# HGRN core of a two-model block stack: query/key pairs rotated before they are normalised, and packed scores

## The chip, the cores and the metric

One core of one Trainium2 chip runs the whole program as one launch. The metric is the device time of a launch in microseconds. The kernel before took 2794.81 us (median of 3 runs, 2794.39 to 2797.06). One more execution was taken under the profiler; the rows in this document come from it.

## The reference, cut to what matters

The input is 512 tokens of 1024 channels. A first block (gated linear attention, a causal convolution, windowed attention, a feed-forward part) is followed by two layers of a second kind. The change touches only those two layers:

```python
for l in range(2):
    u = rmsnorm(x)
    q, k, v, qi, ki, wi, hq, hf, hi, hg, g_attn, g_hgrn = split(u @ w_in[l])
    q = rope(rmsnorm_per_head(q) * q_norm);  k = rope(rmsnorm_per_head(k) * k_norm)   # 8 heads of 64
    qi, ki = rope(qi), rope(ki)                                # 4 index heads, 1 index key head, of 64
    y_attn = sparse_attention(q, k, v, top 128 keys by sum_h wi_h * relu(qi_h . ki)) @ w_proj_attn
    # HGRN: 4 heads, S_t = diag(f_t) S_(t-1) + k_t v_t^T, o_t = S_t^T q_t
    y_hgrn = (rmsnorm(o) * hgrn_norm * silu(hg)) @ w_proj_hgrn
    x = x + (sigmoid(g_attn) * y_attn + sigmoid(g_hgrn) * y_hgrn) @ w_out
    x = x + ffn(x)
```

In the core of the HGRN, `A[t, s]` = sum over d of `q[t, d] k[s, d] exp(b[t, d] - b[s, d])` for s <= t, with `b` the running sum of the log decay. The norm of a head is a factor per token; a rotation turns the two halves of the head's channels into each other. So rotation and norm can change places, if the gain, which is per channel, is applied inside the rotation.

## The kernel before, in words

Activations are kept transposed, channels on partitions, tokens along the free dimension. Every product with weights is three fp32r matmuls for each 128 x 128 tile (high by high, high by low, low by high), so a panel of 1024 x 256 weights is 48 matmuls of 512 columns. The panels are a fixed list, `weight_panels` (line 180): SP loads panel p into `raw[p % 3]` when the results of panel p-3 are complete (line 874); ScalarE rounds it to `wh` (line 912, in `ahead`, which runs at fixed places of ScalarE's own program and waits for the load there); GpSimd makes `wl` (line 896). All engines run in-order programs written out by hand, and count semaphores.

**The core** (`core`: TensorE line 518, ScalarE line 1026, VectorE line 1493) has eight units, one for each pair of heads and block of 128 tokens. A unit is, in TensorE's order: sums of the log decays of one head (lines 543, 544), sums of the other, the turn of the next unit's logs (523), two transposes (556, to become `kdt` by a ScalarE copy at line 1044), score matmuls of seven levels and of the diagonal (567), the output product (575, 577), and the state product (581). ScalarE exponentiates the sums (1038). VectorE multiplies queries and keys into the decays, level by level (1521), then copies each level's scores under a mask into `attT` (1532), copies the output out (1536) and updates the state (1544). Level l splits the block into pieces of 128 / 2^(l+1) tokens, and only pieces with an odd number have queries of that level. The scores take three banks; level 6 and the diagonal go into the bank of levels 0 and 1, so TensorE waits there for the masked copies of those two.

Into these units a second program is dealt in steps, the side work (`side_core_2`: TensorE 768, ScalarE 1246, VectorE 1897). It has the same 40 steps on all three engines, and five a unit: one between the two sums, two behind the second sums, one behind the scores, one at the unit's end (`core_steps`, line 262; the slot between the sixth and seventh level is empty). On TensorE a step is a quarter of a panel, or a *thin* step:

```python
for j in range(4):                       # two pairs of query heads, two of key heads
    yield from project(uh, ul)           # four steps
    turn(qk_pair[j - 1]); yield          # if j > 0: rotation matrix times the normalised pair before
    mean of squares of pair j; yield
```

For pair j ScalarE copies and squares the projection, divides the sum, and takes logarithm and root in later steps; VectorE makes a Newton step on the root (`newton`, line 1607), multiplies pair and gain (1906) and makes the cosine part (`cosine`, 1803), then, after the turn, the sine part and the sum (`turned`, lines 1811 and 1814). The index queries and the index key with its weights follow, and the two value panels.

**After the core**, TensorE makes index scores, VectorE scores the keys (1830, 1832), and `core_post` (TensorE 644, ScalarE 1084, VectorE 1614) norms and gates the output in two halves. For each half TensorE projects a gate panel (`HG`), sums squares, and does four steps of `merge`; ScalarE takes the SiLU (1091) and the root; VectorE first does 14 rounds of the top-k selection (1842, 1844), then the norm (from 1609). Then attention begins with VectorE's masked logits (1652).

## Time and profile before

| | |
|---|---|
| median of the runs | 2794.81 us (2794.39 to 2797.06) |
| profiled execution | 2796.15 us |
| its span, first to last instruction | 2794.4 us |
| mean granted TensorE clock | 0.97 of 2.4 GHz |
| busy: TensorE, VectorE, ScalarE, GpSimd | 2626.1, 1172.5, 994.9, 1074.0 us |
| HGRN core of layers 0 and 1 | from 1039.1 and 1946.7 us, 196.9 and 198.9 us long |

TensorE's busy time contains the overlap of pipelined matmuls, so the time of a step is read from the start of its first matmul to the start of the next group. A busy share says little here; the waits and the windows say which engine was late.

### The profile page before, as it was taken

What the parts mean: (1) busy time and instruction counts of PE and PEld (TensorE: products, weight loads), DVE (VectorE), ACT (ScalarE), POOL (GpSimd) and SP (SyncE); (2) the same over time, 40 slices, a digit from 0 to 9 for tenths busy, and PEclk for the clock granted to TensorE, in tenths of its full rate; (3) what the DMA queues carried; (4) which work ended last, traced back from release to release, by engine and by line L of the source; (5) the groups of instructions that cost most, each with busy time, mean ns of one, the idle gap of its engine ahead of it and who ended that gap; (6) DMA issues with size and microseconds to landing.
All of it is one profiled execution on the core that took longest, in us unless ns stands there. A gap on an engine that the chain in (4) does not pass through costs nothing.

```text
span 2794.4 us, 30147 instructions
## 1 busy us (share of the span) xinstructions
PE 2626.1 (94%) x12478; PEld 2136.2 (76%) x12478; DVE 1172.5 (42%) x1924; ACT 994.9 (36%) x1152; POOL 1074.0 (38%) x816
## 2 busy tenths in 40 slices
PE   6999999999999979888999999999888899999999
PEld 5887777878888777776687888888767668788887
DVE  5243343365523546668625111133666772521112
ACT  3423443343323444425424222235432542432221
POOL 4323333544545442213244544543221324454452
PEclk8999999999999989999999999999999999999999
DMA  4222212222323221111122323223111212232232
GB/s 148 63 76 76 76 61 76 91 92 94 102 91 98 91 68 46 35 57 61 31 92 92 103 91 106 91 91 91 46 36 42 65 40 91 91 101 95 92 104 76
DMA packets 206707, 221.05 MB, mean 79 GB/s; under 512 B 3713, under 2 KB 197467, under 8 KB 206443
## 3 DMA queue, kind: packets, MB, share of 16 engines
q1 hardware_dynamic: 206064, 218.97, 24.5%
q8 instruction: 99, 1.62, 0.2%
q14 instruction: 37, 0.30, 0.0%
q10 hardware_dynamic: 507, 0.15, 0.0%
HBM read 217.01 MB, written 2.10 MB: 78 GB/s over the span
## 4 chain that ended last, share of the span: by engine, by line
PE 79%; DVE 12%; ACT 7%; DMA 1%; issue 1%; DVEq 0%; SPq 0%; ACTq 0%
PE psum L442 70%; PE psum L567 2%; ACT wh L912 2%; PE psum L684 1%; DVE dec L1521 1%; PE psum L672 1%; DMA raw<-in_w_in 1%; PE psum L663 1%; DVE score L1844 1%; DVE ul L1706 1%; DVE top L1842 1%; DVE ul L1417 1%; ACT dec L1038 1%; DVE merged L1729 1%; DVE normed L1478 1%
## 5 line engine op out<-in xcount | busy, mean ns | idle before, releaser
L896 POOL TENSOR_TENSOR wl<-raw,wh 128x512 fp32r<-128x512 f32 x812 | 1073.8, 1356 | 1694.4 <-ACT wh L912 1694.4
L442 PE MATMUL psum<-uh,wh 128*128 128x512 f32 x2024 | 811.8, 401 | 17.8 <-DVE ul L1706 4.4
L442 PE MATMUL psum<-ul,wh 128*128 128x512 f32 x2024 | 797.9, 394 | 0.0
L442 PE MATMUL psum<-uh,wl 128*128 128x512 f32 x2024 | 797.0, 394 | 0.0
L912 ACT CAST wh<-raw 128x2048 fp32r<-128x2048 f32 (+1 forms) x206 | 387.0, 1879 | 313.5 <-DMA raw<-in_w_ffn_out 117.6
L442 PEld LDWEIGHTS psum<-uh,wh 128*128 128x128 f32 x2024 | 386.8, 191 | 110.0 <-issue 14.5
L442 PEld LDWEIGHTS psum<-uh,wl 128*128 128x128 f32 x2024 | 385.9, 191 | 82.8
L442 PEld LDWEIGHTS psum<-ul,wh 128*128 128x128 f32 x2024 | 386.9, 191 | 79.0 <-issue 1.9
L442 PE MATMUL psum<-fh,wh 128*128 128x512 f32 x528 | 205.4, 389 | 0.0
L442 PE MATMUL psum<-fl,wh 128*128 128x512 f32 x528 | 205.4, 389 | 0.0
L442 PE MATMUL psum<-fh,wl 128*128 128x512 f32 x528 | 205.4, 389 | 0.0
L1748 DVE TENSOR_TENSOR xT<-xT,psum 128x1024 f32<-128x1024 f32 (+1 forms) x48 | 56.0, 1166 | 293.0 <-PE psum L442 292.8
L1794 DVE TENSOR_TENSOR tmp<-tmp,psum 128x1024 f32<-128x1024 f32 x22 | 26.9, 1221 | 358.5 <-PE psum L442 358.4
L442 PE MATMUL psum<-vh,wh 128*128 128x512 f32 x288 | 115.8, 402 | 9.2 <-DVE xT L1959 7.1
L442 PEld LDWEIGHTS psum<-fh,wl 128*128 128x128 f32 x528 | 99.1, 188 | 20.7
L442 PEld LDWEIGHTS psum<-fl,wh 128*128 128x128 f32 x528 | 99.1, 188 | 20.6
L442 PEld LDWEIGHTS psum<-fh,wh 128*128 128x128 f32 x528 | 99.1, 188 | 20.4
L442 PE MATMUL psum<-vh,wl 128*128 128x512 f32 x288 | 113.2, 393 | 0.0
L442 PE MATMUL psum<-wh,uh 128*128 128x256 f32 x320 | 92.6, 289 | 11.9 <-DVE ul L1417 11.9
L442 PE MATMUL psum<-vl,wh 128*128 128x512 f32 x256 | 99.7, 389 | 0.0
L567 PE MATMUL psum<-dec 128*128 128x128 f32 x448 | 66.0, 312 | 31.9 <-DVE attT L1532 18.6
L442 PE MATMUL psum<-brh,wh 128*128 128x512 f32 x224 | 94.2, 420 | 0.0
(314 smaller groups left out, 3343.7 us busy)
## 6 DMA issues: line engine op xcount, KB each, us to landing
raw<-in_w_in SPq DMA_DIRECT2D x78, 1024.0 KB, 5.2
raw<-in_w_ffn_in SPq DMA_DIRECT2D x44, 1024.0 KB, 5.1
raw<-in_w_up SPq DMA_DIRECT2D x22, 1024.0 KB, 5.1
raw<-in_w_ffn_out SPq DMA_DIRECT2D x16, 1024.0 KB, 5.1
raw<-in_w_down SPq DMA_DIRECT2D x8, 1024.0 KB, 5.0
raw<-in_w_out SPq DMA_DIRECT2D x8, 1024.0 KB, 5.1
raw<-in_w_ffn_out SPq DMA_DIRECT2D x8, 768.0 KB, 4.3
raw<-in_w_o SPq DMA_DIRECT2D x4, 1024.0 KB, 5.0
```

The lines of the kernel that those rows point to most:

```text
L442: ins = mm(dst, x, y, start=first and i == 0, stop=last and i == len(todo) - 1)
L567: ins = mm(X[1 + l // 2 % 3][:, c:c + P], lhs, rhs, start=True, stop=True)
L663: ins = mm(X[e][:, 0:(b1 - b0) * P], q[HD * e:HD * (e + 1), p, m * P:(m + 1) * P], kof(2 * p + e)[:, b0 * P:b1 * P], start=True, stop=True)
L672: ins = nc.tensor.transpose(X[2][:, b * P:(b + 1) * P], prob[i % 2][:, e, b * P:(b + 1) * P], ident)
L684: ins = mm(X[3][HD * e:HD * (e + 1), 0:P], vof(2 * p + e, b), probT[:, e, (b - b0) * P:(b - b0 + 1) * P], start=(b == b0), stop=(b == b1 - 1))
L896: ins = nc.gpsimd.tensor_tensor(wl[p % 3][:, w], raw[p % 3][:, w], wh[p % 3][:, w].bitcast(F32), ALU.subtract)
L912: nc.scalar.copy(wh[p % 3][:, 0:nk * width], raw[p % 3][:, 0:nk * width]).then_inc(S.hi_done, 1)
L1038: fn(dec[:, i, :, :].rearrange("p (b l) t -> p b (l t)", b=3), X4[:, 1:4, 0:3 * P], ACT.Exp).then_inc(S.dec_done, 1)
L1417: v.tensor_tensor(dst, src, high.bitcast(F32), ALU.subtract).then_inc(sem, 1)
L1478: v.scalar_tensor_tensor(normed[:, c % 2, :], xT[:, c, :], g(c), scale[:], ALU.mult, ALU.mult).then_inc(S.n_normed, 1)
L1521: ins = v.tensor_tensor(e[:, :, :, part, :], e[:, :, :, part, :], x[:, :, :, part, :], ALU.mult)
L1748: v.tensor_tensor(x, x, src, ALU.add).then_inc(pair_free[(n.q - 1) % 2], 1)
```

## The change

- The key-index panel is projected first in the side work, then the four pairs, the index queries, the two value panels, and as the last one the first of the two gate panels of `core_post`, which for these layers no longer projects it (`gated`); two of the four `merge` steps stand ahead of its first sum.
- A pair is handled unnormalised: ScalarE squares it (into a tile of its own, `qksq`) and copies it; one thin step on TensorE makes the mean of squares and the turn, the latter with a rotation matrix that has the gain multiplied in (`rot_gain`, made once a layer from a part of `const` that is no longer needed). VectorE takes the sine part in the step of the thin work, adds gain times cosine in the last step of a unit, and multiplies the root in the first step of the next.
- On ScalarE mean, weight cast, logarithm, root and square are one step (`rooted`).
- Scores of a level are computed for the odd pieces only, 64 columns for each head, and all eight results have places of their own in the three banks; the diagonal comes first; the masked copies go level by level to the odd pieces only. TensorE signals after levels 1, 3 and 6 and waits for all copies once.

```diff
-                  C_AQ, C_AQ + 256, C_AK, C_AK + 256, C_IQ, C_IK, C_AV, C_AV + 256, C_HG):
+                  C_IK, C_AQ, C_AQ + 256, C_AK, C_AK + 256, C_IQ, C_AV, C_AV + 256, C_HG):
-SIDE_CORE_2 = 4 * 6 + 4 + 4 + 2 * 4
+SIDE_CORE_2 = 2 + 4 * 5 + 4 + 5 + 5 + 4
+LEVEL_ENDS = (1, 3, 6)
+        def odd_blocks(x, l):
+            w = P >> (l + 1)
+            return x.rearrange("p (g two w) -> p g two w", two=2, w=w)[:, :, 1, :]
+        def level_scores(l):
+            w = P >> (l + 1)
+            at = l + 2 if l < 4 else l + 4
+            return X[1 + at // 4][:, P * (at % 4):P * (at % 4 + 1)].rearrange("p (h g w) -> p h g w", h=2, w=w)
 # TensorE, core
-                        if l == 6:
-                            take_on(side, core_steps(total, u, 2))
-                            pe.wait_ge(S.pairs_done, t.up(S.pairs_done))
...
+                    for i in range(2):
+                        h = 2 * hp + i
+                        ins = mm(X[1][:, i * P:(i + 1) * P], gk[:, h, tok], gq[:, h, tok], start=True, stop=True)
+                    for l in range(LEVELS):
+                        pe.wait_ge(S.lev_ready, t.up(S.lev_ready))
+                        for i in range(2):
+                            ins = mm(level_scores(l)[:, i, :, :], dec[:, i, l, :], odd_blocks(dec[:, i, l, :], l),
+                                     start=True, stop=True)
+                        if l in LEVEL_ENDS:
+                            ins.then_inc(S.att_done, 1)
 # TensorE, side work
+                yield from project(uh, ul, (0,))
+                keys = n.q - 1
                 for j in range(4):
                     yield from project(uh, ul)
                     mine = n.q - 1
-                    if j > 0:
-                        turn(qk_pair[j - 1])
-                        yield
                     dst = new_pair()
+                    pe.wait_ge(S.squared, t.up(S.squared))
+                    for i in range(2):
+                        ins = mm(dst[:, i, :], blk, qksq[:, i, :], start=True, stop=True)
+                    ins.then_inc(S.pair_full, 1)
                     pe.wait_ge(pair_free[mine % 2], mine // 2 + 1)
+                    turn(qk_pair[j], rot_gain[j // 2])
                     yield
 # ScalarE, side work
+                def squared(j):
                     src = next_pair()
...
+                    fn(qksq[:], src, ACT.Square).then_inc(S.squared, 1)
+                    fn(qk_pair[j], src, ACT.Copy).then_inc(pair_free[(n.q - 1) % 2], 1)
+                    ahead()
+                def rooted(j):
+                    src = next_pair()
+                    mean = n.q - 1
...
+                    mean_square(tmp[1][:], src, 1.0 / HD, pair_free[mean % 2])
+                    ahead()
+                    next_pair()
+                    ahead()
+                    act.wait_ge(pair_free[mean % 2], mean // 2 + 1)
+                    logarithm(tmp[0][:], tmp[1][:])
+                    inverse_root(tmp[0][:]).then_inc(S.r_root, 1)
+                yield from passed(2)
+                for j in range(4):
+                    yield from wait_steps(3)
+                    squared(j)
+                    yield
+                    rooted(j)
+                    yield
...
+                yield from wait_steps(3)
+                act.wait_ge(S.r_normed, t.up(S.r_normed))
+                silu_gate()
 # VectorE, core
-                        v.copy_predicated(attT[:], mask, src).then_inc(signal, 1)
+                        w = P >> (l + 1)
+                        mask = odd_blocks(pairmask[:, l, :], l).unsqueeze(1).to_broadcast([P, 2, P // (2 * w), w])
+                        dst = attT[:].rearrange("p h (g two w) -> p h g two w", two=2, w=w)[:, :, :, 1, :]
+                        v.copy_predicated(dst, mask, level_scores(l)).then_inc(signal, 1)
 # VectorE, side work
+                for j in range(4):
+                    next_pair()
+                    sine(tmp[2][:])          # sine table times the turned pair, from PSUM
+                    yield
+                    yield from wait_steps(2)
+                    cosines(j)               # pair * gain * cosine, then + sine part
+                    yield
+                    normed(j)                # newton(), then pair * root
+                    if j < 3:
+                        next_pair()
+                        yield
 # TensorE, core_post
+                    before = 2 if gated and j == 0 else 0
+                    take_on(side, before)
+                    if j or not gated:
+                        finish(project(uh, ul))
...
-                    take_on(side, side_steps[j])
+                    take_on(side, side_steps[j] - before)
```

## Rows read from the trace of the kernel before

**Rows 1.** Page, part 4: shares of the chain that ended last.
```profile
PE 79%; DVE 12%; ACT 7%; DMA 1%; issue 1%; DVEq 0%; SPq 0%; ACTq 0%
```
**Rows 2.** Windows (us; PE, PEld, DVE, ACT, POOL busy; PEclk): cores, units 3, 5, 0, stages after.
```profile
1039.10:1236.00 196.90, 174.77 (x970) 148.68 (x970) 117.68 (x265) 73.78 (x73) 47.53 (x36) 0.93 0.13 40
1946.70:2145.60 198.90, 174.96 (x969) 148.69 (x970) 118.49 (x265) 73.78 (x73) 47.48 (x36) 0.93 0.13 39
1111.10:1130.80 19.70, 19.43 (x105) 15.59 (x105) 13.66 (x34) 13.40 (x13) 5.31 (x4) 1.00 0.18 54
1156.20:1184.90 28.70, 22.29 (x113) 17.95 (x112) 17.49 (x36) 4.81 (x5) 6.93 (x4) 0.94 0.12 37
...
1039.10:1061.40 22.30, 21.07 (x107) 18.05 (x108) 8.47 (x28) 7.07 (x8) 4.19 (x4) 0.93 0.15 44
...
1236.00:1295.50 59.50, 50.68 (x220) 38.90 (x220) 47.07 (x108) 33.69 (x31) 15.20 (x12) 0.97 0.29 89
2145.60:2206.80 61.20, 52.40 (x221) 40.13 (x220) 47.04 (x107) 33.66 (x31) 15.21 (x12) 0.94 0.28 86
```
**Rows 3.** Waits of PE in the first core: total, times, longest.
```profile
PE psum L567 <- DVE attT L1532: 8.4, 3, 2.9
PE psum L567 <- DVE dec L1521: 6.7, 3, 2.4
PE psum L765 <- DVE ak L1906: 3.8, 1, 3.8
...
PE psum L779 <- ACT tmp L1266: 1.2, 1, 1.2
```
**Rows 4.** Timeline of PE in the first core: start us, us.
```profile
1051.44 3.29 PE L567 MATMUL psum<-dec 128*128 128x128 f32 x28
...
1054.93 0.48 PE L442 MATMUL psum<-uh,wh 128*128 128x512 f32 x1
...
1130.83 0.34 PE L543 MATMUL psum<-summask,lth 128*128 128x384 f32 x1
...
1131.89 0.39 PE L442 MATMUL psum<-uh,wh 128*128 128x512 f32 x1
...
1134.62 0.34 PE L543 MATMUL psum<-summask,lth 128*128 128x384 f32 x1
...
1207.58 0.36 PE L442 MATMUL psum<-wh,uh 128*128 128x256 f32 x1
...
1210.53 0.34 PE L543 MATMUL psum<-summask,lth 128*128 128x384 f32 x1
...
1211.67 0.41 PE L794 MATMUL psum<-const,tmp 4*128 4x4 f32 x4
```
**Rows 5.** Groups by form, ScalarE and VectorE: busy us, mean ns, idle before.
```profile
L912 ACT CAST wh<-raw 128x2048 fp32r<-128x2048 f32 x12 | 22.8, 1899 | 13.0 <-DMA raw<-in_w_in 13.0
L1038 ACT ACTIVATE dec<-psum 128x1152 f32<-128x1152 f32 x16 | 18.1, 1131 | 33.9 <-PE psum L544 33.8
L1075 ACT ACT_TABLE_LOAD x6 | 7.7, 1283 | 0.1
...
L1075 ACT ACTIVATE tmp<-tmp 128x1024 f32<-128x1024 f32 x6 | 6.4, 1061 | 0.1
...
L1532 DVE COPY_PREDICATED attT<-pairmask,psum 128x256 f32<-128x256 uint8 x64 | 28.5, 445 | 5.3 <-PE psum L567 3.4
...
L1521 DVE TENSOR_TENSOR dec<-dec,gk 128x128 f32<-128x128 f32 x56 | 15.8, 282 | 0.0
```
**Rows 6.** Page, part 6: a panel's DMA, median us from issue to landing.
```profile
raw<-in_w_in SPq DMA_DIRECT2D x78, 1024.0 KB, 5.2
```
**Rows 7.** Timeline of the stage after the first core.
```profile
1262.27 1.23 DVE L1609 TENSOR_TENSOR tmp<-tmp 128x1024 f32<-128x1024 f32 x1 [3.54 <-ACT tmp L1082]
...
1287.86 1.22 DVE L1609 TENSOR_TENSOR tmp<-tmp 128x1024 f32<-128x1024 f32 x1
...
1296.06 0.80 PE L663 MATMUL psum<-ak,aq 64*128 64x128 f32 x4 [7.01 <-DVE stat L1652]
```

More of the change, by code:

```diff
@@ L360, in build_program @@
         bias3 = at("bias3", 20, [P, 4 * P])
-        iwT = tmp[0][HD:HD + 4, 0, :]
+        iwT = at("iwT", 65, [P, T])[HD:HD + 4, :]
+        ikcos = at("ikcos", 67, [P, T])
+        qksq = at("qksq", 69, [P, 2, T])
+        rot_gain = [const[:, K_DIST + i * P:K_DIST + (i + 1) * P] for i in range(2)]
         prob = [tmp[0], tmp[1]]
@@ L783, in side_core_2 @@
                 queries = n.q - 1
-                turn(qk_pair[3])
-                yield
-                yield from project(uh, ul, (0,))
-                keys = n.q - 1
-                turn(iq, queries)
-                yield
-                yield from project_tokens()
                 dst = new_pair()
@@ L797, in side_core_2 @@
                 yield from project_tokens()
+                pe.wait_ge(pair_free[queries % 2], queries // 2 + 1)
+                turn(iq, rot)
+                yield
+                yield from project_tokens()
+                yield from project(uh, ul)
             pe.wait_ge(S.ident_in, 16)
@@ L1088, in core_post @@
                     fn(tmp[1][:], gq[:, heads, :], ACT.Square).then_inc(S.g_square, 1)
-                    src = next_pair()
-                    act.wait_ge(S.pair_full, n.q)
-                    fn(tmp[0][:], src, ACT.Silu).then_inc(pair_free[(n.q - 1) % 2], 1)
-                    ahead()
+                    if j or not gated:
+                        silu_gate()
                     act.wait_ge(S.g_summed, t.up(S.g_summed))
@@ L1612, in newton, with core_post @@
                 dve.wait_ge(S.dve_chain, t.up(S.dve_chain))
-            def core_post(g, same, side, side_steps, selection=None):
+            def core_post(g, same, side, side_steps, selection=None, gated=False):
                 for j in range(2):
@@ L1935, in side_core_2 @@
                 yield
-                turned(iq[:])
-                cosine(ik[:].unsqueeze(1))
+                yield from wait_steps(2)
+                v.tensor_tensor(ikcos[:], ik[:], cosT[:], ALU.mult).then_inc(S.dve_chain, 1)
+                dve.wait_ge(S.dve_chain, t.up(S.dve_chain))
                 yield
-                yield from passed(4)
+                yield from passed(1)
+                for j in range(4):
+                    next_pair()
+                    sine(tmp[2][:])
+                    yield
+                    yield from wait_steps(2)
+                    cosines(j)
+                    yield
+                    normed(j)
+                    if j < 3:
+                        next_pair()
+                        yield
+                src = next_pair()
+                dve.wait_ge(S.pair_full, n.q)
+                v.tensor_copy(iq[:], src).then_inc(pair_free[(n.q - 1) % 2], 1)
+                dve.wait_ge(pair_free[(n.q - 1) % 2], (n.q - 1) // 2 + 1)
+                yield
                 src = next_pair()
@@ L1942, in side_core_2 @@
                 v.tensor_scalar(iw[:].rearrange("p m h -> p (m h)"), src[:, 1, 0:4 * NT], 1.0 / 16, None, ALU.mult)
-                v.tensor_tensor(tmp[3][:, 0, :], src[:, 0, :], sinT[:], ALU.mult).then_inc(pair_free[(n.q - 1) % 2], 1)
+                v.tensor_tensor(ik[:], src[:, 0, :], sinT[:], ALU.mult).then_inc(pair_free[(n.q - 1) % 2], 1)
                 dve.wait_ge(pair_free[(n.q - 1) % 2], (n.q - 1) // 2 + 1)
-                v.tensor_tensor(ik[:], tmp[2][:, 0, :], tmp[3][:, 0, :], ALU.add).then_inc(S.rope_done, 1)
+                v.tensor_tensor(ik[:], ik[:], ikcos[:], ALU.add).then_inc(S.dve_chain, 1)
+                dve.wait_ge(S.dve_chain, t.up(S.dve_chain))
+                yield
+                yield from wait_steps(2)
+                cosine(iq[:])
+                yield
+                yield from passed(1)
+                sine(iq[:])
+                v.tensor_tensor(iq[:], iq[:], tmp[2][:], ALU.add).then_inc(S.rope_done, 1)
                 dve.wait_ge(S.rope_done, t.up(S.rope_done))
@@ L1948, in side_core_2, with gains_of, turns_with_gains @@
                 yield from passed(4)
+                yield from passed(4)
+            def gains_of(l):
+                return small[:, 9 + l:10 + l], vech[:, V_KN + l:V_KN + l + 1]
+            def turns_with_gains(l):
+                for by, g in zip(rot_gain, gains_of(l)):
+                    v.tensor_scalar(by, rot, g, None, ALU.mult).then_inc(S.dve_chain, 1)
+                    dve.wait_ge(S.dve_chain, t.up(S.dve_chain))
             v.memset(ones[:], 1.0).then_inc(S.dve_chain, 1)
```

137 lines of the change are left out of this document (43 added, 94 removed).

## The prediction

> **What bounds the kernel now.** The page's chain first: nearly four fifths of the span is TensorE work and 12% VectorE [rows 1], so time is won only where TensorE waits or runs at its lower clock. The windows then say where: the two HGRN cores last 196.9 and 198.9 us with a granted clock of 0.93, and their eight units are uneven: 19.7 us in unit 3, at clock 1.00, but 28.7 us in unit 5 [rows 2]. The waits of the first core name the causes: 8.4 us for `attT` (level 6 may not overwrite the bank of levels 0 and 1 before their masked copies are out), 6.7 us for `dec` (the level products come late), 3.8 us for `ak` (a turn waits for the normalised pair) and 1.2 us for the squares [rows 3]. That is 20 us, and the low clock behind the longer waits adds to it. The stage after the core (59.5 and 61.2 us, [rows 2]) is another matter: it ends with TensorE waiting 7.0 us for VectorE's first attention logits [rows 7]. VectorE sets its end.
>
> **Prices.** A weight step (12 matmuls of 512 columns) takes 1134.62 - 1131.89 = 2.73 us; a token step 1210.53 - 1207.58 = 2.95; the sums of one head 1131.89 - 1130.83 = 1.06; the sixteen score matmuls (32 f32 instructions of 128 columns) 1054.93 - 1051.44 = 3.49, or 0.109 each [rows 4]. A mean or a turn is four f32 instructions of 512 columns: 4 x 4 x 0.109 = 1.72 rounded down by the gaps.
>
> **Part 1, packed scores.** Fourteen of the sixteen matmuls (28 instructions) stream 64 columns in place of 128. From below an instruction would take half of 0.109, 0.055; from above 0.109 again, if something other than the stream bounds it. The nearest row loads 128 columns of weights and streams only four: four instructions in 0.41 us, of which the last's own 0.20 is not spacing, so about 0.07 to 0.085 each [rows 4]. I take 0.083: 28 x 0.026 = 0.7 us a unit, bounds 0 and 1.5. On VectorE eight masked copies of 256 (0.445 us, [rows 5]) become one of 256 and seven of 128; the level products of 128 take 0.28 [rows 5], so with some 0.03 between them the copies go from 3.8 to 2.7 us, with bounds of 0 and 3 us saved. All scores now fit three banks, so the wait before level 6 goes. Next is the wait before the output product, with a weight step ahead of it to cover the copies.
>
> The page "TensorE: Matmul & The Clock Gate" of the Trainium skill, section "LDWEIGHTS (loading the stationary operand)", gives P / 1.2 ns for P columns, 107 ns for 128: by it the packed instruction stays near 0.107 us and the 0.7 us goes. The four-column row, at 0.07 to 0.085 with 128 weight columns, speaks against it. That case is a rival below.
>
> **Part 2, rotate first.** Per pair VectorE still does six operations of 1024 (sine, two for the cosine, two of Newton, one product, 1.23 each [rows 7]), but the turn no longer waits for a normalised pair: both mean and turn need only ScalarE's square and copy of the raw pair. Five of VectorE's six now stand after the unit's state update and before the next decays: 5 x 1.26 = 6.3 us, while TensorE does a weight step, the sums, a weight step and the sums again, over 7.5 us, and ScalarE a decay (1.13, [rows 5]) before VectorE is needed. So they are hidden and the `dec` wait goes; without that cover they would cost what unit 5 now loses. Only the sine stands before the masked copies.
>
> Take a middle unit (2 to 4), with time from the end of the projection of its pair. ScalarE: square to 1.0, copy to 2.0 (an operation of 1024 takes some 1.0 to 1.06, [rows 5]), second decay to 3.1, log copy to 3.4, mean to 4.5. TensorE: sums and log turns to 1.2, mean to 2.9, turn to 4.6. The next projection needs the mean's buffer, free at 4.5: no wait. VectorE: products from about 4.5 to 7.3, sine to 8.6, copies done near 11.3. TensorE: weight step to 7.35, transposes and scores to 10.4, weight step to about 13.2; the scores are ready. **The added wait** is on ScalarE: mean, weight cast, logarithm, root and square are now one step that stands before the copy of `kdt`, for which the output product waits, and behind that the state, `gq` and the next unit. The cast needs a panel issued at the pair's end and landed 5.2 us later [rows 6]: 5.3 to 7.2 (1.90, [rows 5]); then two table loads of 1.28 and three operations of 1.06 [rows 5] to 13.0; `kdt` at 13.4. TensorE wants it at 13.2: 0 to 0.7 us, taken as nil after rounding the steps up. In unit 1 there is one more cast, since the key panel has no thin pair behind it, and it stands ahead of the second decay: the mean's buffer comes free at 6.3 in place of 4.6, a wait of 1.7 us.
>
> The page "ScalarE: Activation LUTs" of the Trainium skill, section "What ACT_TABLE_LOAD costs", adds a drain of about 1.38 us to each load; `kdt` would then come 2.8 us later, in four units of two layers some 20 us. Here the load's row is 1.28 us and the activation behind it idled 0.1 us in six together [rows 5], so this case's trace does not bear the drain out and the measurement decides.
>
> **Part 3, order of panels.** The index key panel comes first and the first gate panel moves into the core. The same 40 steps are dealt 1, 2, 0, 1, 1 a unit; 34 are now full and six thin, where 30 were full and ten thin. SP's DMAs (5.2 us, [rows 6]) and the casts stay as many panels ahead as before, and a panel lasts TensorE over 11 us (four weight steps), some 20 within the core, so the order as such costs nothing. In the last units the casts that waited for their DMA stood ahead of the second decay (that is the `dec` wait of 2.4 us); now they stand behind it. The two small gain multiplications before the core run while VectorE is idle. I bound them by 0 and 0.5 us a layer and take 0.
>
> **The core's sum.** Unit 3 is the clean base: 19.7, less its 0.3 of idle time = 19.4 us with three weight steps, one mean, one turn.
> Unit 0: two thin steps less (3.44), two weight steps more (5.46), packing 0.7 and the missing state product 0.45 less, and 1.1 more for the low clock at the start (before, 22.3 us [rows 2] against 19.4 - 1.7 + 2.7 - 0.45 + 1.2 of wait = 21.2): 21.4. Unit 1: one weight step more, -0.7, -0.45, +1.7 wait: 22.7. Units 2 to 4: 19.4 + 2.73 - 0.7 = 21.4, three times 64.3. Unit 5: a thin step of 1.2, one weight and three token steps (11.6) for 11.6 of before: 19.8. Unit 6: a turn and four token steps for three weight steps and two thin: 20.6. Unit 7: one token and four weight steps: 20.9. Together 169.7 against 196.9: **-27 us**. In the second core 198.9 against some 171: **-28**. That includes the gate projection that has moved in (4 x 2.73 = 10.9 us a layer).
>
> **The stage after.** It loses that projection but hardly the time. ScalarE evicts the gate (1.0) and casts (1.9) before the index scores, so the first scores come 1.9 us later. VectorE's fourteen selection rounds ended at 1262.27 - 3.54 = 1258.7, 22.7 us after the core; with the change they end at 24.6. In the kernel before it starts on the norm at 26.3, after a wait of 3.5 for ScalarE [rows 7]. ScalarE's root, with two steps ahead of its sum and not four, is there by 21.4, so VectorE saves 1.6 us in layer 0. In layer 1 the same stage is 1.7 longer, so 3.3. The rest is unbroken VectorE work (at the second norm it did not wait at all [rows 7]). TensorE merely waits some 16 us where it waited 7. So -1.6 and -3.3.
>
> Sum: -27 - 28 - 5 = -60 us. The profiled execution took 2796.15 us (span 2794.4), 1.3 above the median shown, so 2736 in it and **2735 us** as a median.
>
> **Rivals.**
> (A) The packed matmul stays at 0.109 us: for it, that weights are loaded once for each instruction; against it, the four-column row. 0.7 x 16 units = +11: 2746.
> (B) ScalarE's long step is late: `kdt` 3 us later than worked out. Each wait near 3 us has been followed by a stretch at the low clock (window of unit 5, 0.94; whole core 0.93), worth some 1.4 us. In 8 units 4.4 us: +35, 2770. For it: the slack is nil. Against: every term is a row.
> (C) Slower. The packed operand skips every other block, down to every other element, and TensorE reads it badly. For it: no row of before streams such an operand. Against: VectorE's products on the same blocks take 0.28 at every level [rows 5]. At 0.33 us an instruction it costs 28 x 0.25 = 7 us a unit, +112: 2847. It decides from 3.8 us a unit on (0.22 an instruction), where the whole gain is gone.
> (D) Better than forecast: half price for the packed instruction and no low clock at all in the core, 16 x 0.8 + 6 = -19: 2716.
>
> **Chances.** Forecast 0.62 (its own range 2724 to 2750), A 0.14, B 0.14, C 0.04, D 0.06. The range 2714 to 2768 leaves out C, most of B's upper half and a little of D. No change means within 0.2% (5.6 us), about what a measurement of this kernel can tell. Only C reaches to no gain: faster 0.95, same 0.01, slower 0.04.
>
> **What would show it.** Right: no wait for `attT` at the scores or for the turned pairs, units of 20 to 23 us, clock near 1 in the core, core near 170 us; score bursts near 2.8 us; a stage after it that ends 58 us behind the core with a TensorE wait there of 9 us or more. Wrong: waits at the output product with `kdt` as releaser (B), score bursts of 3.5 (A) or far more (C), or a stage after the core that shrinks by the 10.9 us moved. The number fails if the cores are not at least 20 us shorter each.

## The result, and the profile after

The changed kernel took 2763.84 us (median of 4 runs, 2760.5 to 2766.03) beside 2794.6 us (4 runs, 2788.82 to 2797.06) for the kernel before: ratio 0.9892, 95% interval 0.9873 to 0.991. It is faster, by some 31 us where 60 were forecast. The profiled execution took 2762.72 us (span 2760.9).

The page of the changed kernel: busy time and share of the span of each engine, then the chain that ended last [rows 1].

```profile
PE 2613.3 (95%) x12478; PEld 2125.0 (77%) x12478; DVE 1161.3 (42%) x1928; ACT 994.4 (36%) x1152; POOL 1075.2 (39%) x816
...
PE 82%; DVE 12%; ACT 5%; issue 1%; DMA 0%; DVEq 0%; SPq 0%; ACTq 0%
```

Windows of the changed kernel with the columns of [rows 2] (the last two numbers are the busy share of the DMA engines and GB/s): the two cores, units 1 and 2 of the first, and both stages after a core, up to the second query-key product.

```profile
1035.50:1217.42 181.92, 176.65 (x1018) 151.78 (x1018) 109.15 (x265) 74.50 (x74) 48.02 (x36) 0.97 0.16 49
1930.02:2111.90 181.88, 176.61 (x1018) 151.70 (x1018) 109.16 (x265) 74.53 (x74) 47.95 (x36) 0.97 0.16 49
1057.92:1088.53 30.61, 25.75 (x114) 20.59 (x112) 18.15 (x31) 14.96 (x14) 10.48 (x8) 0.89 0.12 35
1088.53:1110.55 22.02, 22.02 (x117) 17.95 (x116) 15.07 (x36) 13.33 (x13) 5.01 (x4) 1.00 0.16 49
...
1217.42:1279.47 62.05, 46.62 (x173) 33.23 (x173) 49.91 (x111) 33.29 (x30) 15.36 (x12) 0.85 0.22 68
2111.90:2173.95 62.05, 45.34 (x172) 32.85 (x173) 49.94 (x111) 33.28 (x30) 15.36 (x12) 0.88 0.22 68
```

The cores are 15.0 and 17.0 us shorter (forecast 27 and 28). Unit 2 has no idle time at all and a granted clock of 1.00 (units 3 and 4 are like it, 22.1 and 22.0 us), so there the change did what it says. Most of the shortfall shows in two places: unit 1 is 30.6 and 30.5 us long in the two layers, with twice the GpSimd work of its neighbours (eight pieces for four), and the stage after is no shorter. To the same end, a second query-key product, it was 1296.06 - 1236.00 = 60.1 us before [rows 2, 7] and 61.8 in the second layer; now it is 62.05 in both. 3.6 us less arose ahead of the first core, in code the change does not touch, and 0.2 less elsewhere. The 3.6 may be chance: the changed kernel and its variants with the same code there start that core anywhere from 1034.0 to 1038.2 us. Sum: -15.0 - 17.0 + 2.0 + 0.3 - 3.8 = -33.5, the difference of the two spans.

Waits of TensorE in the first core of the changed kernel, as [rows 3] (total us, times, longest): the 8.4 us for `attT` and the wait for the turned pair are gone, one new group is there.

```profile
PE psum L580 <- DVE dec L1536: 3.5, 3, 1.9
PE psum L559 <- DVE ltl L1515: 2.1, 1, 2.1
PE psum L458 <- ACT tmp L1085: 1.3, 1, 1.3
PE psum L590 <- DVE attT L1550: 0.4, 1, 0.4
```

All three waits for `dec` stand in unit 1. Two timelines of the changed kernel (start us, duration us) show why: VectorE's products, and GpSimd.

```profile
1068.41 1.52 DVE L1530 TENSOR_TENSOR dec<-dec,gq 128x256 f32<-128x256 f32 x1
1069.86 1.38 DVE L1536 TENSOR_TENSOR dec<-dec,gq 128x128 f32<-128x128 f32 x1
1071.17 1.36 DVE L1536 TENSOR_TENSOR dec<-dec,gk 128x128 f32<-128x128 f32 x1
...
1076.27 0.28 DVE L1536 TENSOR_TENSOR dec<-dec,gk 128x128 f32<-128x128 f32 x1
```
```profile
1065.71 10.48 POOL L909 TENSOR_TENSOR wl<-raw,wh 128x512 fp32r<-128x512 f32 x8 [13.22 <-ACT wh L925]
```

GpSimd runs from 1065.7 to 1076.2. Each of VectorE's five products of 128 columns that start inside it takes 1.35 to 1.38 us, the first after its end 0.28 again. The cast that ScalarE makes between its two Exp in this unit alone starts GpSimd just ahead of the products, and a second cast of the same unit doubles GpSimd's run, four pieces for each cast.

The stage after, ScalarE and VectorE of the changed kernel from the core's end at 1217.4:

```profile
1217.50 1.28 ACT L1300 ACT_TABLE_LOAD   x1 [10.09 <-PE psum L458]
1218.80 1.02 ACT L1300 ACTIVATE tmp<-psum 128x1024 f32<-128x1024 f32 x1
1219.72 1.89 ACT L925 CAST wh<-raw 128x2048 fp32r<-128x2048 f32 x1
1221.51 0.60 ACT L1123 ACTIVATE tmp<-psum 128x512 f32<-128x512 f32 x1
```
```profile
1222.21 0.89 DVE L1839 TENSOR_SCALAR score<-tmp,iw 128x256 f32<-128x256 f32 x1 [6.62 <-ACT tmp L1123]
1223.13 1.36 DVE L1841 SCALAR_TENSOR_TENSOR score<-tmp,iw,score 128x256 f32<-128x256 f32 x1
```

Table load, Silu and cast all stand ahead of the first ReLU of the index scores, and the GpSimd run that the cast starts stretches the first scores. TensorE idles 15.4 us in this stage at a granted clock of 0.85, but only 6.4 us of that is the last wait, for the attention logits; the rest is spread over waits for scores, gate and norm, and 2.1 us for GpSimd's low words.

Unit 0 shows the two engines meeting the other way round. Here VectorE's products are already running when the cast releases GpSimd: GpSimd's first piece, then the last product of 128 columns.

```profile
1045.52 3.28 POOL L909 TENSOR_TENSOR wl<-raw,wh 128x512 fp32r<-128x512 f32 x1 [5.83 <-ACT wh L925]
```
```profile
1047.38 0.29 DVE L1536 TENSOR_TENSOR dec<-dec,gk 128x128 f32<-128x128 f32 x1
```

No product is stretched, and the piece takes 3.28 us instead of 1.28: it is held until the products are over. So it matters which engine is running first.

### The profile page after: what moved, and what is told of

It is laid out like the page before. It is cut to its first block, busy times and chain, and to the rows that moved or that the text cites. A ratio compares the mean times of both kernels' runs of the same rounds, so it can differ in the third digit from the quotient of the medians.

```text
span 2760.9 us, 30113 instructions
## 1 busy us (share of the span) xinstructions
PE 2613.3 (95%) x12478; PEld 2125.0 (77%) x12478; DVE 1161.3 (42%) x1928; ACT 994.4 (36%) x1152; POOL 1075.2 (39%) x816
## 4 chain that ended last, share of the span: by engine, by line
PE 82%; DVE 12%; ACT 5%; issue 1%; DMA 0%; DVEq 0%; SPq 0%; ACTq 0%
PE psum L458 72%; PE psum L580 2%; ACT wh L925 1%; DVE score L1853 1%; DVE top L1851 1%; PE psum L702 1%; PE psum L690 1%; PE psum L681 1%; DVE ul L1726 1%; DVE ul L1432 1%; DVE dec L1536 1%; PE psum L559 1%; DVE score L1841 1%; PE psum L560 1%; DVE merged L1749 1%
## 5 line engine op out<-in xcount | busy, mean ns | idle before, releaser
L458 PE MATMUL psum<-wl,uh 128*128 128x256 f32 x320 | 91.7, 286 | 0.0
L458 PE MATMUL psum<-wh,ul 128*128 128x256 f32 x320 | 91.6, 286 | 0.0
```

Source lines behind the costliest of these rows:

```text
L458: ins = mm(dst, x, y, start=first and i == 0, stop=last and i == len(todo) - 1)
```

## The experiments

Times are medians; "the changed kernel" is 2763.8 us. The letters of the theories are those of the expectation that stands above each result.

**The cast one unit earlier.** `ahead(done=1)` casts the next panel one step sooner, at the end of unit 0. In ScalarE's side steps:

```diff
                 for j in range(4):
-                    yield from wait_steps(3)
+                    yield from wait_steps(2)
+                    if j == 0:
+                        ahead(done=1)
+                    yield
                     squared(j)
```

> ScalarE's cast of the fourth weight panel counted from the index panel (the first half of the keys) is issued at the end of unit 0 instead of in unit 1 between the two Exp of the decays; all else stays. Theory A (GpSimd's eight subtractions, which that cast starts, run beside VectorE's level products in unit 1 and stretch each from 0.28 to 1.36 us): unit 1 falls from 30.6 to 22 to 23 us in both layers, the products go back to 0.28 to 0.42, and the kernel takes some 16 us less, about 2748. Theory B (unit 1 is long because its mean and its turn wait for ScalarE's Square, Copy and mean eviction, which are late for reasons of their own): unit 1 keeps 28 us or more, less than 5 us in all.

2746.15 us (2742.71 to 2749.6), ratio to before 0.9831 (0.9815 to 0.9847): 17.7 less than the changed kernel. Unit 1 of the first layer and a product in it:

```profile
1061.85:1083.48 21.63, 21.63 (x113) 17.51 (x112) 10.92 (x31) 13.34 (x13) 4.99 (x4) 1.00 0.16 49
```
```profile
1070.19 0.28 DVE L1539 TENSOR_TENSOR dec<-dec,gq 128x128 f32<-128x128 f32 x1
```

9.0 us less there, and 8.9 in the second layer; VectorE's busy time in the unit is 10.92 for 18.15. Of the 9.0, 4.9 had been TensorE idle (30.61 - 25.75) and 4.1 the same work at a lower clock (0.89 for 1.00), behind its waits. Theory A holds so far, B is out. (The eight pieces of the expectation are two panels; the cast that moved starts the first four, and four are left in unit 1.) The run moves two things at once, though: ScalarE's 1.9 us and GpSimd's start.

The profiled execution also shows a cost elsewhere: unit 0 of the first layer is 25.4 us instead of 22.4. There GpSimd got in between the running products, and four of them took 1.35 to 1.38 us:

```profile
1046.47 1.48 POOL L909 TENSOR_TENSOR wl<-raw,wh 128x512 fp32r<-128x512 f32 x1 [5.83 <-ACT wh L925]
```
```profile
1046.72 1.38 DVE L1539 TENSOR_TENSOR dec<-dec,gk 128x128 f32<-128x128 f32 x1
```

The early cast is not the reason: in the second layer of this run unit 0 is 22.1 us, and three traces without the early cast show the same thing (see the end of the next part).

**The casts late in every unit.**

```diff
-                    ahead()
                     next_pair()
-                    ahead()
                     act.wait_ge(pair_free[mean % 2], mean // 2 + 1)
```

> The suspected cost multiplied: the casts that units 1 to 4 make after both Exp, in the step that evicts the mean, are left to the next unit's Square step, between its two Exp, as it is in unit 1 now. The same work, the same panels. Theory A: units 2, 3 and 4 (perhaps 5) become some 29 to 31 us each as unit 1 is, that is 7 to 8 us more per unit, 42 to 60 us in both layers, 2806 to 2824. Theory B or C: the second Exp is late by the cast's 1.9 us in each, 1.9 us x 3 x 2 = at most 12 us, 2764 to 2776.

2769.84 us (2766.33 to 2771.6), ratio 0.9914 (0.9898 to 0.9931): 6 more, not 42 to 60. A miss, and an instructive one. Units 1 and 2, then GpSimd and VectorE in unit 1:

```profile
1058.35:1082.31 23.96, 22.12 (x113) 17.38 (x112) 13.86 (x31) 13.17 (x13) 5.37 (x4) 1.00 0.14 44
1082.31:1106.74 24.43, 22.61 (x117) 17.80 (x116) 18.00 (x36) 13.17 (x13) 5.37 (x4) 1.00 0.15 44
```
```profile
1066.14 5.37 POOL L909 TENSOR_TENSOR wl<-raw,wh 128x512 fp32r<-128x512 f32 x4 [13.20 <-ACT wh L925]
```
```profile
1070.28 1.38 DVE L1534 TENSOR_TENSOR dec<-dec,gq 128x128 f32<-128x128 f32 x1
1071.58 0.28 DVE L1534 TENSOR_TENSOR dec<-dec,gk 128x128 f32<-128x128 f32 x1
```

Units 2 to 4 pay 2.4 us each, but unit 1, which kept its early cast, fell from 30.6 to 24.0. With one panel GpSimd ends at 1071.5, after three stretched operations, when TensorE is just done with its weight step; only the second panel, right behind the first, carries the overlap through the products TensorE waits for. What costs is how far GpSimd's run reaches into the products. I had read unit 1 as the price of one cast.

**GpSimd waits, the casts stay.** A first try at the same question, in which GpSimd forms only the last piece of the first keys' panel, gave no time. Here it forms all of them, but later.

```diff
                 pool.wait_ge(S.hi_done, p + 1)
+                if p in HELD:                      # the first keys' panel of a layer
+                    pool.wait_ge(S.lev_ready, PRODUCTS[HELD.index(p)])   # unit 1's products
```

> Both of ScalarE's casts of unit 1 stay where they are in the changed kernel; only GpSimd waits, for the panel of the first keys, until VectorE has finished unit 1's level products. So the cast's 1.9 us on ScalarE remain and the overlap goes. Theory A (the overlap of GpSimd's pieces and the products is what costs; the run with the late casts paid only 2.4 us a unit because with one panel in unit 1 GpSimd has ended, 1071.5, after three stretched products, and in the changed kernel two panels run one behind the other until 1076.2): the products take 0.28 to 0.42 us, unit 1 is 22 to 24 us instead of 30.6, the kernel 13 to 17 us less than the changed one, about 2749. Theory C (the second Exp, made late by the cast, and the blocked ScalarE cost): unit 1 stays at 28 us or more, the time within 5 us of 2764.

2749.14 us (2746.84 to 2751.42), ratio 0.9833 (0.9818 to 0.9848): 14.7 less. Unit 1, with ScalarE's casts where they were:

```profile
1060.64:1083.83 23.19, 21.86 (x114) 17.42 (x112) 10.92 (x31) 14.96 (x14) 9.99 (x8) 1.00 0.15 46
```

The same eight pieces, moved behind VectorE's products, give back 7.4 of the 9.0 us. The cast's own 1.9 us on ScalarE is worth the other 1.6. That parts A from C.

**The gate projection back in the stage after.**

```diff
-                yield from project(uh, ul)         # TensorE, last in the core's side steps
+                for _ in range(4):
+                    yield
...
-                core_post(side, SIDE_POST_2, True)
+                core_post(side, SIDE_POST_2)
```

> The first gate projection goes back from the core (its last four projection steps, 10.9 us) to the stage after it; the core's last slots stay empty. If the moved projection buys nothing behind the core (my reading: the stage after is 62.05 us with it, 60.07 and 61.7 before the change, so it is carried by waits there): the core is 10.9 us shorter in each layer, 181.9 to 171, the stage after stays within 3 us of 62, and the kernel is 16 to 22 us shorter, 2742 to 2748. If the projection is real work that has to be done in either place (rival): the stage after is 10.9 longer, 73 us, and the time is within 3 us of 2764.

2756.36 us (2750.29 to 2759.68), ratio 0.9865 (0.9847 to 0.9883): 7.5 less by the medians, 12.4 in the profiled executions. Unit 7, then the stage after, then TensorE's waits in unit 7:

```profile
1197.13:1212.69 15.56, 11.53 (x84) 10.78 (x82) 6.88 (x26) 3.66 (x4) 0.00 (x0) 0.94 0.22 68
1212.69:1273.86 61.17, 52.61 (x221) 40.09 (x221) 48.37 (x114) 33.30 (x30) 15.20 (x12) 0.92 0.23 69
```
```profile
PE psum L590 <- DVE attT L1550: 2.0, 1, 2.0
PE psum L572 <- ACT dec L1052: 2.0, 1, 2.0
```

The stage takes the 10.9 us of work back and is 0.9 us shorter than without it. So the projection was free there. In the core it costs only 5.8 (181.9 to 176.1), as it had covered two waits of 2.0 in unit 7 and the lower clock behind them (0.94 here); I had put down all 10.9. The time lies between the two expectations, the mechanism is the first.

**The gate served.** The projection stays in the core.

```diff
                 act.wait_ge(S.r_normed, t.up(S.r_normed))
-                silu_gate()
+                fn(tmp[1][:, 0, 0:1], tmp[1][:, 0, 0:1], ACT.Silu)    # brings the table in
+                silu_gate(cast=False)
...
                     if j or not gated:
                         silu_gate()
+                    else:
+                        ahead()
```

> The gate projection stays in the core. ScalarE loads the Silu table ahead of that projection's end (by a Silu of one element) and casts no panel right behind the Silu, but after the square of the core's output, behind the index scoring. Theory A (the stage after did not get its 1.6 and 3.3 us because table load, cast and the GpSimd run that the cast starts stand in front of and beside the index scoring): the first ReLU comes some 3 us after the core's end instead of 4.1, scoring is over at 10 to 11 us instead of 14.5, selection starts and ends 3.5 to 4.5 us earlier, and the kernel takes 6 to 9 us less than the changed one, 2755 to 2758. Rival (the selection's own work or the panels bound the stage, so a cast made late comes back as a wait of TensorE for its low words): within 2 us of 2764.

2753.28 us (2752.04 to 2753.79), ratio 0.9847 (0.983 to 0.9863): 10.6 less, a little over what was expected. ScalarE and VectorE from the core's end at 1217.6, and the stage:

```profile
1217.63 1.02 ACT L1303 ACTIVATE tmp<-psum 128x1024 f32<-128x1024 f32 x1 [8.53 <-PE psum L458]
1218.55 0.59 ACT L1125 ACTIVATE tmp<-psum 128x512 f32<-128x512 f32 x1
```
```profile
1219.25 0.35 DVE L1843 TENSOR_SCALAR score<-tmp,iw 128x256 f32<-128x256 f32 x1 [3.48 <-ACT tmp L1125]
1219.64 0.48 DVE L1845 SCALAR_TENSOR_TENSOR score<-tmp,iw,score 128x256 f32<-128x256 f32 x1
```
```profile
1217.60:1273.51 55.91, 40.09 (x173) 29.83 (x173) 46.92 (x111) 31.91 (x29) 15.11 (x12) 0.92 0.24 75
```

The first ReLU starts 0.95 us after the core's end instead of 4.1, the first score operations take 0.35 and 0.48 instead of 0.89 and 1.36, and the stage is 55.9 us instead of 62.05. The run moves the table load, the cast and GpSimd's run together, so it does not say what each is worth.

**The scores unpacked.**

```diff
-                            ins = mm(level_scores(l)[:, i, :, :], dec[:, i, l, :], odd_blocks(dec[:, i, l, :], l), ...)
+                        if l == 6:
+                            take_on(side, core_steps(total, u, 2))
+                            pe.wait_ge(S.pairs_done, t.up(S.pairs_done))
+                            ins = mm(X[1 + l // 2 % 3][:, c:c + P], lhs, rhs, start=True, stop=True)
```

> The scores alone are undone: TensorE streams all 128 columns of each level, VectorE copies 128x256 under the mask eight times, the last pair of levels waits for the first copies again, and one projection step goes back between the sixth and seventh level. Rotation and order of steps stay as changed. Theory A (a score instruction takes 0.109 us with 64 streamed columns as with 128, so packing bought TensorE nothing; VectorE's copies, 3.6 against 2.8 us a unit, are covered by the projection step): within 3 us of 2764. Theory F (my forecast's price, 0.7 us a unit, was right and something else in the units ate it): 11 us more, 2775. A larger loss, 2780 or more, would say that the order of waits that packing allowed was worth more than its columns.

2771.73 us (2769.74 to 2776.93), ratio 0.9917 (0.9901 to 0.9932): 8 more, between the two. The price per instruction is settled by the bursts of score instructions in unit 3 here and unit 2 of the changed kernel (32 instructions with the diagonal, up to the next weight step):

```profile
1127.53 3.29 PE L583 MATMUL psum<-dec 128*128 128x128 f32 x28
1130.66 0.61 PE L583 MATMUL psum<-gq,gk 128*128 128x128 f32 x4
1131.03 0.48 PE L458 MATMUL psum<-uh,wh 128*128 128x512 f32 x1
```
```profile
1100.16 0.61 PE L576 MATMUL psum<-gq,gk 128*128 128x128 f32 x4
1100.60 3.24 PE L580 MATMUL psum<-dec 128*128 128x64 f32 x28
1103.65 0.48 PE L458 MATMUL psum<-uh,wh 128*128 128x512 f32 x1
```

3.50 us with 128 columns, 3.49 with 64, and units 2 to 4 are 22.1 us either way. The 8 us are elsewhere: unit 6 is 24.5 us instead of 21.3 in both layers, where TensorE waits 2.1 us for `attT` before level 6, unit 5 is 0.9 us longer, and unit 0 is 28.5 and 23.7 instead of 22.4. So packing paid, through the wait it removed and not through its columns. (The 28.5 is one of the cases in which GpSimd got in between the products, four of 1.35 to 1.39 us, so part of unit 0's share is chance. Unit 0 is also 22.3 to 26.5 us in runs whose unit 0 is the same code on TensorE.)

**What sets a score instruction.** Levels 0 and 1 with 64 weight columns, 2 and 3 with 32 streamed, 4 to 6 as changed. Half of the scores of levels 0 and 1 and three quarters of those of levels 2 and 3 are left out, so only the instructions' spacing is read from this run.

```diff
+                            if l < 2:
+                                ins = mm(X[1 + at // 4][0:64, c:c + 64], dec[:, i, l, 0:64], dec[:, i, l, 64:128], ...)
+                            elif l < 4:
+                                ins = mm(X[1 + at // 4][:, c:c + 32], dec[:, i, l, :], dec[:, i, l, 96:128], ...)
```

> One look at the price of a score instruction, with three shapes in each unit: levels 0 and 1 load 64 weight columns and stream 64 (the other half of their scores is left out), levels 2 and 3 load 128 and stream 32 (three quarters left out), levels 4 to 6 load 128 and stream 64 as changed. If loading the 128 weight columns sets the 0.109 us: levels 0 and 1 fall to 0.05 to 0.08, levels 2 and 3 stay at 0.109. If the streamed columns set it: levels 2 and 3 fall to 0.06 or less, levels 0 and 1 stay. If it is a fixed cost of an instruction: all three stay at 0.109.

One execution, 2763.31 us. TensorE in unit 0, the three shapes in order:

```profile
1048.38 0.68 PE L584 MATMUL psum<-dec 128*64 128x64 f32 x8
1048.99 1.08 PE L586 MATMUL psum<-dec 128*128 128x32 f32 x8
1049.91 1.53 PE L588 MATMUL psum<-dec 128*128 128x64 f32 x12
1051.25 0.48 PE L458 MATMUL psum<-uh,wh 128*128 128x512 f32 x1
```

From start to start: (1048.99 - 1048.38) / 8 = 0.076 us with 64 weight columns, 0.92 / 8 = 0.115 with 128 and 32 streamed, 1.34 / 12 = 0.112 with 128 and 64. The weight columns set it. The page "TensorE: Matmul & The Clock Gate" of the Trainium skill, section "LDWEIGHTS (loading the stationary operand)", puts the weight load at P / 1.2 ns for P columns. The estimate by it, 107 ns for 128 columns, is close to the 0.109 to 0.115 us here; for 64 columns the estimate is 53 ns where this run has 76.

**GpSimd in shorter pieces.**

```diff
-LOW_PIECE = 512
+LOW_PIECE = 256
```

> The changed kernel with GpSimd's subtractions cut into pieces of 256 columns instead of 512, eight a panel instead of four; all else stays. It asks how VectorE is held up in unit 1, where each product beside GpSimd took 1.36 us, just as long as one piece of GpSimd. Theory P (the two engines take turns, one instruction each, so a product waits out one piece): the products beside GpSimd take 0.65 to 0.8 us, twice as many get through in the same time, and unit 1 is 27.5 to 29.5 us instead of 30.6; the kernel some 2 to 6 us less per unit count, 2757 to 2761, if GpSimd's own work does not grow. Theory R (they share a rate, so that a product beside GpSimd takes about 1.1 to 1.4 us whatever the pieces): unit 1 stays at 30 us or more, and the time at 2762 to 2768 or above.

2747.68 us (2745.91 to 2753.25), ratio 0.9843 (0.9825 to 0.9861): 16 less than the changed kernel, far more than either theory gave. The products of unit 1 and GpSimd beside them:

```profile
1059.74 0.83 DVE L1536 TENSOR_TENSOR dec<-dec,gq 128x128 f32<-128x128 f32 x1
1060.49 0.83 DVE L1536 TENSOR_TENSOR dec<-dec,gk 128x128 f32<-128x128 f32 x1
```
```profile
1056.57 11.95 POOL L909 TENSOR_TENSOR wl<-raw,wh 128x256 fp32r<-128x256 f32 x16 [12.63 <-ACT wh L925]
```

A product now takes 0.83 us, and one starts every 0.75, just as GpSimd's pieces do (11.95 / 16 = 0.75). That is theory P: with GpSimd running first, they take turns, instruction by instruction. But unit 1 hardly gains (29.9 and 30.5 us, where it was 30.6 and 30.5), since GpSimd's run, longer by 1.5 us, now covers twelve of the fourteen products. The gain is outside the units: the first core starts at 1026.4 instead of 1035.5 (the changed kernel and its variants with pieces of 512 have 1034.0 to 1038.2). Of the 9.1 us, over 3 are there ahead of the layer's opening norm and over 5 arise in it. There VectorE's operation at L1432 (128x512) beside GpSimd took up to 1.67 us and takes up to 1.12, and TensorE's wait for it falls from 11.6 to 5.9:

```profile
L1432 DVE TENSOR_TENSOR ul<-normed,uh x48: 691/693/1671, 48.4 to 2414.2; 128x512 fp32r<-128x512 f32 x48
```
```profile
L1432 DVE TENSOR_TENSOR ul<-normed,uh x48: 691/693/1116, 47.3 to 2399.0; 128x512 fp32r<-128x512 f32 x48
```

(The changed kernel first, then this one: minimum, median and maximum ns.) There is another side to it: the feed-forward part's operations of 1024 on the same line are more often stretched (median 1.78 for 1.23 us).

**Together.** Three combinations, five rounds each; their edits are those above.

```diff
 early and back:    ahead(done=1) in unit 0; gate projection in the stage after
 waits and back:    pool.wait_ge(S.lev_ready, ...); gate projection in the stage after
 early and served:  ahead(done=1) in unit 0; Silu table ahead, cast behind the scoring
```

> Two of the edits together: the cast of the first keys' panel at the end of unit 0, and the gate projection back in the stage after the core. If their gains add (the first works in unit 1, the second behind unit 7): 2763.8 less 17.7 and 7.5 by the medians, 2739; by the stretches in the traces (unit 1 9.0 less per layer, from unit 7 to the second query-key product 6.5 less) 31 less, 2733. If the clock takes some back, as TensorE idles 4 us a layer in unit 7 without the gate: 2740 to 2744.

2735.19 us (2732.24 to 2738.1), ratio 0.9798 (0.978 to 0.9815). The gains add: it lies between the two sums of the expectation.

> As the run before, but the overlap is kept off by GpSimd's wait instead of the earlier cast, so ScalarE's cast still stands between the two Exp of unit 1: unit 1 23.2 us instead of 21.6, so 3 us more than the run before in both layers, 2736 to 2743.

2742.7 us (2739.14 to 2744.42), ratio 0.9821 (0.9803 to 0.9838): 7.5 more than the run before where 3 were expected. Unit 1 (23.2 us) explains 3.2; in the profiled execution unit 0 of the first layer was 26.5 for 23.5, again with four stretched products.

> The early cast and the served gate together: the gate projection stays in the core, ScalarE's table is loaded ahead and the cast made behind the index scoring. If the gains add: 2763.8 less 17.7 and 10.6 by the medians, 2735.5, level with putting the projection back (within 4 us); TensorE's clock is not lowered in unit 7. If putting the projection back is better by more than 4 us, then the 6 us that it holds in unit 7 are worth more than the cover it gives.

2734.66 us (2731.77 to 2736.83), ratio 0.9795 (0.9777 to 0.9813). Level with the first, as expected. That the cover in unit 7 and the cost of the projection there cancel is a reading of the two times, not measured by itself.

**All three edits.** The last combination with `LOW_PIECE = 256`.

> The early cast, the served gate and GpSimd's pieces of 256 columns together. If the gain of the shorter pieces lies outside the stretches that the other two edits mend (the trace of the run with pieces of 256 has unit 1 at 29.9 and 30.5 us, as before, and reaches the first core 9 us sooner, in code that neither edit touches), it adds: 2734.7 less 16, about 2719. If it came from the same overlaps (unit 1 and the index scoring), little is left to gain: 2728 to 2735.

2722.08 us (2718.59 to 2724.35), ratio 0.9746 (0.973 to 0.9763), so 12.6 us less again, and the shortest of all: 41.8 us under the changed kernel, 72 under the one before. The shorter pieces mostly add: 12.6 of the 16 us.

## Why the prediction was right in direction and half off in size

The measured 2763.8 us lies outside the forecast's own range (2724 to 2750). It lies inside the wide one (2714 to 2768) only because that was stretched for rival B, whose late `kdt` did not occur: that is luck. By the prediction's own sign the number fails, as the cores are 15.0 and 17.0 us shorter and not at least 20.

**What bounds the kernel: right.** Cores and stages behaved as read; the `attT` waits [rows 3] fell from 8.4 to 0.4 us, the turn no longer waits, and VectorE's operations of 1024 between the units held nobody up: units 2 to 4 have no idle time and a clock of 1.00.

**Part 1: the size was wrong, rival A true.** The packed instruction was put at 0.083 us; it takes 0.109 to 0.112 from start to start (3.05 us for 28 in unit 2, 1.34 for 12 in the run with three shapes), and the bursts are 3.5 us, the sign of rival A. The seven units of the first core other than unit 1 came out 0.3 to 1.0 us above their terms (22.4 for 21.4, 22.05 for 21.4 three times, 20.2 for 19.8, 21.3 for 20.6, 21.2 for 20.9), 4.3 in all; in the second core the rest is 3.2. The 0.7 us a unit that was booked is not there. The row that was held against the Trainium skill's rule, [rows 4], streams four columns against weights of four rows, and why it is quicker stays open. What the packing did buy, the wait before level 6, I had listed without a price of its own; the unpacked run puts wait and packing together at 8 us.

**Part 2: right but for unit 1.** ScalarE's long step was never late: no wait for `kdt` appeared, rival B is out. In unit 1 the added cast was seen, and its wait of 1.7 us for the mean's buffer is there with 1.33.

**Part 3, "the order as such costs nothing", is the step that failed.** It priced the casts on ScalarE and the panels' arrival, and never asked what a cast sets off: four or eight GpSimd pieces, each of which, where GpSimd runs first, holds up one operation of VectorE that reads two tensors from SBUF. Unit 1 was put at 22.7 us and took 30.6 and 30.5, 7.9 and 7.8 too much, and the two runs that take that overlap away win back 17.7 us (together with the cast's own 1.9 us between the two Exp) and 14.7 us (the overlap alone). The sign was in the trace of before too. One line of its first core, over the products (minimum, median, maximum ns):

```profile
L1521 DVE TENSOR_TENSOR dec<-dec,gq x56: 277/284/1345, 1048.2 to 1225.6; 128x128 f32<-128x128 f32 x56
```

The mean row that I used [rows 5] was 282 ns for the other operand and hid a maximum of 1345. The `dec` waits of 6.7 us [rows 3], which I put down to a late second Exp, were part late Exp and part this: all three stand in units whose first three products (some 3 us more together than in the others) run beside GpSimd, and the units whose products run alone have no such wait. The page "SBUF — State Buffer" of the Trainium skill, section "SBUF: two separate sides", has the rule: VectorE and GpSimd arbitrate for one pair of ports, an exclusive lock for a whole instruction, which a VectorE operation takes that has two SBUF inputs or runs in a two-port mode. The traces of unit 1 agree: products 1.35 us beside pieces of 1.34, 0.83 beside pieces of 0.78, while the sine (which reads one operand from PSUM, 1.22 us), the masked copies and the top-8 operations kept their durations beside GpSimd. Cited in time, it would have been a rival with some 16 us.

**The stage after: the term was off by 3.6 us in each layer** (-1.6 and -3.3 forecast, +2.0 and +0.3 measured). Two things were left out: the Silu's table load (1.28 us), which starts at 1217.5, only when the projection is full, and again the GpSimd run beside the first scores. With both mended the stage is 55.9 us, shorter than the forecast 58.5; what each of the two costs is not shown. The wait for the logits at its end was to be 9 us or more and is 6.4. That its end is VectorE's, not TensorE's, was right: 10.9 us of TensorE work put back into it changed it by -0.9.

**The sum.** Unit 1 cost 15.7 us, the score price and small roundings 7.5, the stages 7.2, and 3.8 outside cores and stages were not forecast. The forecast's parts add to 60.1 before rounding: 60.1 - 15.7 - 7.5 - 7.2 + 3.8 = 33.5, the difference of the two spans. With the early cast and the served gate the kernel takes 2734.66 us, the core 172.8 and the stage 56.0 where 169.7 and 58.5 were forecast. The forecast was of a kernel with two scheduling slips fewer than the one that ran; that the number is met so closely is partly chance, since the score term stays wrong.

**The first unit.** It varies from 22.1 to 28.5 us between runs, and the traces say where most of that comes from. In every one GpSimd's run starts 0.7 to 0.8 us after the first product of 128 columns. In 22 of the 26 cases (two layers of the changed kernel and of twelve variants) the first piece is held until the last product is over, no product is stretched, and the unit is 22.1 to 23.7 us. In the other four (25.4, 25.3, 28.5 and 26.5 us) GpSimd gets in after the fourth or fifth product, four products take 1.35 us or more, and TensorE waits 0.8 to 1.4 us for `dec`.

Open: what decides whether GpSimd gets in between two running products; the spread from 22.1 to 23.7; and how much of the 12.6 us of the shorter pieces lies in which stage. None was tried.

## What to carry to other kernels

When an engine's step is moved, follow what it releases on every other engine and lay that run beside the work that stands there in the new place: a cast that costs 1.9 us moved a GpSimd run of 10.5 us onto the critical products. Look at the maximum of a group and not only its mean: 284 ns with a maximum of 1345 is a conflict that only the schedule keeps rare. Look also at which of the two engines runs first: GpSimd's run of eight pieces released just ahead of the products cost 7.4 us in unit 1, while a run released behind the first products mostly cost nothing. Before cutting the streamed columns of a small f32 matmul, ask whether the weight columns set its price.

## What the runs showed of the hardware that was not expected

- VectorE operations with two SBUF operands and GpSimd's take turns one for one where GpSimd's run is under way first (unit 1): 1.35 us a product of 128 columns beside pieces of 512 columns, 0.83 beside pieces of 256, 0.28 alone. GpSimd's piece beside them took 1.34 us on average instead of 1.28 (5.01 us for four alone, 10.48 for eight beside).
- Where the products run first (unit 0), GpSimd's first piece was held until the last product was over (3.28 us for a piece of 512) and the products kept their 0.28 to 0.30 us, in 22 of 26 cases; in four GpSimd got in.
- Halving GpSimd's pieces raised its busy time from 1075 to 1217 us and shortened the kernel by 16 and, on the better version, 12.6 us.
- A packed f32 operand that skips every other column costs no more than a plain one: 28 instructions of levels 0 to 6 in 3.24 us, against 3.29 for unpacked ones. The weight columns set the price of both, so a stream slowed by up to that much would not show.
